# Seven half-size products in place of eight in the second mixer's output projection

## What is computed

```python
y = rms_norm(y * jax.nn.silu(z), ssm_norm_g)
mix = jnp.concatenate([y, att], axis=-1) @ w_out
x = x + g1 * mix
h = rms_norm(x, norm_ffn_g[i]) * (1 + sc2) + sh2
x = x + g2 * swiglu(h, ffn_w_gate[i], ffn_w_up[i], ffn_w_down[i])
```

## Time and profile before

| | us |
|---|---|
| runs shown, median of 3 | 1491.78 |
| lowest and highest of them | 1487.80, 1494.51 |
| profiled execution | 1488.53 |
| its span, first to last instruction | 1486.8 |
| output projection, first to last matmul (824.04 to 907.82) | 83.8 |
| mean granted clock of TensorE | 0.98 of full speed |

### The profile page before, as it was taken

The page is one execution under the profiler, slowest core; times in us unless marked ns, Lnnn a source line. Parts: engine busy times, 40 slices in busy tenths (PEclk is TensorE's granted clock), DMA queues, the critical chain, the costliest instruction groups (busy, mean ns, idle before and its releaser), DMA issues. The chain is left out here.

```text
span 1486.8 us, 18918 instructions
## 1 busy us (share of the span) xinstructions
PE 1396.1 (94%) x7609; PEld 1031.1 (69%) x7609; DVE 765.1 (51%) x1333; ACT 248.3 (17%) x530; POOL 254.1 (17%) x342
## 2 busy tenths in 40 slices
PE   5999999988677999999999999999999999999997
PEld 1877655644344888778888888777766868777774
DVE  2458775423214676844452113788763963544532
ACT  2121212000002212313343101000002022000001
POOL 5078010000002000643345104000021000000000
PEclk9999999999989999999999999999999999999999
DMA  9976788999999688847764454988843633445430
GB/s 349 314 256 236 257 339 356 378 414 418 417 417 309 226 293 289 286 123 187 172 134 136 148 162 155 330 322 334 311 170 114 203 102 114 147 165 170 155 128 28
DMA packets 176054, 355.56 MB, mean 239 GB/s; under 512 B 7289, under 2 KB 137040, under 8 KB 158560
## 3 DMA queue, kind: packets, MB, share of 16 engines
q1 hardware_dynamic: 166720, 313.64, 59.5%
q0 software_dynamic: 9248, 40.71, 9.4%
HBM read 352.58 MB, written 1.74 MB: 238 GB/s over the span
## 5 line engine op out<-in xcount | busy, mean ns | idle before, releaser
L1789 PE MATMUL PS<-HT,ring 128*128 128x256 f32 x1152 | 258.3, 382 | 0.1
L1789 PEld LDWEIGHTS PS<-HT,ring 128*128 128x128 f32 x1152 | 215.4, 190 | 36.0 <-issue 7.9
L2604 PE MATMUL PS<-ring,hid 128*128 128x512 f32 x320 | 143.5, 592 | 0.0
L2604 PEld LDWEIGHTS PS<-ring,hid 128*128 128x128 f32 x320 | 60.8, 190 | 60.3 <-issue 58.4
L2598 PE MATMUL PS<-HT,ring 128*128 128x256 f32 x464 | 101.6, 379 | 0.0
L2598 PEld LDWEIGHTS PS<-HT,ring 128*128 128x128 f32 x464 | 87.8, 190 | 11.8
L1969 PE MATMUL PS<-ring,y_T 128*128 128x256 f32 x384 | 83.3, 379 | 0.0
L1969 PEld LDWEIGHTS PS<-ring,y_T 128*128 128x128 f32 x384 | 72.9, 190 | 9.9
L1262 PE MATMUL PS<-ring_extra,slot_rows 128*32 128x256 f32 x576 | 54.2, 429 | 27.1 <-DMA ring_extra<-in_expert_w_gate 7.1
L1539 DVE TENSOR_TENSOR X<-X,PS 128x1024 f32<-128x1024 f32 x14 | 17.1, 1221 | 110.9 <-PE PS L1315 110.9
L2627 PE MATMUL PS<-ada_stage,half_sums 128*128 128x256 f32 x288 | 68.1, 379 | 0.0
(11 more groups left out here) (598 smaller groups left out, 2167.0 us busy)
## 6 DMA issues: line engine op xcount, KB each, us to landing
ring<-in_hy_w_in SPq DMA_DIRECT2D x40, 1024.0 KB, 7.6
ring_extra<-in_w_ada SPq DMA_DIRECT2D x24, 1024.0 KB, 7.9
ada_stage<-in_ada_w POOLq DMA_DIRECT2D x24, 1024.0 KB, 7.7
ring<-in_ffn_w_gate SPq DMA_DIRECT2D x22, 1024.0 KB, 5.7
ring<-in_ffn_w_up SPq DMA_DIRECT2D x22, 1024.0 KB, 5.8
ring<-in_ffn_w_down SPq DMA_DIRECT2D x22, 1024.0 KB, 5.6
ring_extra<-in_expert_w_down SPq DMA_DIRECT2D x18, 1024.0 KB, 22.9
ring_extra<-in_expert_w_up SPq DMA_DIRECT2D x18, 1024.0 KB, 20.2
```

Source lines behind the costliest of these rows:

```text
L1789: mm = pe.matmul(dst, w[:, k, half * P:(half + 1) * P], HT[:, k, :], start=(k == 0), stop=(k == KT - 1))
L2604: mm = pe.matmul(PS[:, 4 + 2 * i + h, :], hid[:, par, f, i * P:(i + 1) * P], w[:, f, h * 512:(h + 1) * 512], start=first and f == 0, stop= ...
```

## The change

The projection is done by column pieces twice as wide (`pc` = 0, 1, of 512 columns) and for each group of 1024 rows as a 2x2 block product: the rows' two token halves against the two 512-row halves, and the two 256-column halves of the weights. Seven products `P1` to `P7` of one 128x512 by 512x256 block each take the place of the eight of the plain way. What follows from that:

- DVE sums blocks of `YT` (`sum_y`, four operations of 128x512 for each group, three times) and blocks of the two weight tiles of a group (`sum_out`, four operations of 128x1024, six times; one result is written over half of a ring slot).
- PE does, for each `pc`, the attention group's products by themselves (`out_half(pc, 0)`, 28 matmuls) and those of groups 0 and 1 together, product by product (`out_half(pc, 1)`, 56 matmuls). Each product has half a PSUM bank; part 0 takes banks 2 to 5, part 1 banks 6, 7, 0 and 1.
- The four matmuls for the squares stand between the first two parts, and their result in bank 1.
- ACT copies `P1` of each part. DVE adds the products up: `combine_a` for the attention group, with gate and addition to `X`; `combine_b` for the other two, with the token's scale and the gate in one operation, in four pieces of 128x256. ACT squares `X` piece by piece.
- PE waits for the sums (`y_summed`, `out_summed`) and, before it reuses banks, for DVE to have read them (`read_a`, `read_b`). Tiles of the second column half are asked for in another order, and slots come free at other places (`used`).
- Three of `sum_y`'s and `sum_out`'s calls stand on DVE among steps 37 and 38, ahead of the multiplications of `y`; the others behind step 39.

```diff
-    segment("hy_out", [kp(hy_out[g * D:(g + 1) * D, :], c * CW) for c in range(4) for g in (2, 0, 1)])
+    OUT_GROUPS = (2, 0, 1)
+    segment("hy_out", [kp(hy_out[g * D:(g + 1) * D, :], (2 * pc + h) * CW) for pc in range(2)
+                       for g, h in ((2, 0), (2, 1), (0, 0), (1, 0), (0, 1), (1, 1))])
...
-        ta = W[:].rearrange("p a b -> p (a b)")[:, 0:2 * 512].rearrange("p (a n) -> p a n", a=2)
+        ta = W[:].rearrange("p a b -> p (a b)")[:, 0:4 * CW].rearrange("p (i n) -> p i n", i=TT)
+        partial = rx_zb[:, 0:6 * CW].rearrange("p (a n) -> p a n", a=6)
+        out_sum0 = sb(scope, "out_sums", [P, 3, 4, CW])
+        out_sum = (out_sum0[:], carve(rows_q, 0, [3, 4, CW]), carve(x_scores, 0, [3, 4, CW]))
+        y_sum = (KTT[:].rearrange("p a s -> p (a s)").rearrange("p (j k n) -> p j k n", j=4, k=4),
+                 V[:].rearrange("p i n -> p (i n)").rearrange("p (j k n) -> p j k n", j=4, k=4),
+                 carve(cum_bias, 0, [4, 4, P]))
...
+        SEVEN = ("P2", "P1", "P6", "P5", "P3", "P7", "P4")
+        OUT_ORDER = {(0, 0): SEVEN, (0, 1): ("P2", "P1", "P3", "P7", "P5", "P6", "P4"), (1, 0): SEVEN, (1, 1): SEVEN}
+        HOMES = ({"P2": (2, 0), "P1": (2, 1), "P6": (3, 0), "P5": (3, 1), "P3": (4, 0), "P7": (4, 1), "P4": (5, 0)},
+                 {"P2": (6, 0), "P1": (6, 1), "P6": (7, 0), "P5": (7, 1), "P3": (0, 0), "P7": (0, 1), "P4": (1, 0)})
+        OUT_PIECES = ((0, 0), (0, 1), (1, 1), (1, 0))
+        def out_items(n):
+            pc, gi = n // 3, n % 3
+            return tuple(OUT + 6 * pc + at for at in ((0, 1), (2, 4), (3, 5))[gi])
+
+        def y_block(g, i, h):
+            return YT[:, g * KT + 4 * h:g * KT + 4 * h + 4, i * P:(i + 1) * P]
...
-                for c in range(4):
-                    n = base + NP + 3 * c
-                    arrive(pe, n)
-                    if c == 0:
-                        pe.wait_ge(moved_att, KT)
-                        pe.wait_ge(evac, NP - 1)
-                    elif c == 1:
-                        pe.wait_ge(evac, NP)
-                    else:
-                        pe.wait_ge(part_a, c - 1)
-                    for i in range(TT):
-                        mm = out_half(n, 2, i, c % 2, True, True)
-                    mm.then_inc(used, 1)
-                    if c == 0:
-                        pe.wait_ge(copied, 2 * ATT_SLOTS)
-                    if c >= 2:
-                        pe.wait_ge(summed_out, c - 1)
-                    if c == 0:
-                        pe.wait_ge(gained, 8)
-                    for i in range(TT):
-                        for g in range(2):
-                            if i == 0:
-                                arrive(pe, n + 1 + g)
-                            mm = out_half(n + 1 + g, g, i, 6 + c % 2, g == 0, g == 1)
-                            if i == TT - 1:
+                def out_half(pc, part):
+
+                    order = OUT_ORDER[pc, part]
+                    sets = [3 * pc + gi for gi in ((0,), (1, 2))[part]]
+                    operands = {name: [] for name in order}
+                    for n in sets:
+                        g, ys, ws = OUT_GROUPS[n % 3], y_sum[n % 3], out_sum[n % 3]
+                        w0, w1 = (w_slot(item) for item in out_items(n))
+                        for name, lhs, rhs in (("P2", y_block(g, 0, 1), w0[:, 4:8, :]), ("P1", y_block(g, 0, 0), w0[:, 0:4, :]),
+                                               ("P6", ys[:, 1], ws[:, 1]), ("P5", ys[:, 0], ws[:, 0]),
+                                               ("P3", ys[:, 3], w1[:, 4:8, :]), ("P7", ys[:, 2], w1[:, 0:4, :]),
+                                               ("P4", y_block(g, 1, 1), ws[:, 2])):
+                            operands[name] += [(lhs[:, k, :], rhs[:, k, :]) for k in range(4)]
+                    summed = [name for name in order if name not in ("P2", "P1", "P3")][0]
+                    free = order[max(order.index("P3"), order.index("P7")) + 1]
+                    for n in sets:
+                        arrive(pe, out_items(n)[0])
+                    pe.wait_ge(y_summed, sets[-1] % 3 + 1)
+                    for name in order:
+                        if name == "P3":
+                            for n in sets:
+                                arrive(pe, out_items(n)[1])
+                        if name == summed:
+                            pe.wait_ge(out_summed, sets[-1] + 1)
+                        if (pc, part, name) == (0, 1, "P4"):
+                            pe.wait_ge(meaned, 1)
+                        pairs_in = operands[name]
+                        for j, (lhs, rhs) in enumerate(pairs_in):
+                            mm = pe.matmul(out_home(part, name), lhs, rhs, start=(j == 0), stop=(j == len(pairs_in) - 1))
+                            if name in (summed, free) and j < len(sets):
                                 mm.then_inc(used, 1)
-                    if c == 0:
-                        pe.wait_ge(sq_added, 8)
-                        for i in range(TT):
-                            for a in range(2):
-                                mm = pe.matmul(PS[:, 2, i:i + 1], sq_sum[:, a * S + i * P:a * S + (i + 1) * P], ones[:, 0:1],
-                                               start=(a == 0), stop=(a == 1))
-                        mm.then_inc(msum, 1)
+                        mm.then_inc(out_products, 1)
+                pe.wait_ge(moved_att, KT)
+                pe.wait_ge(copied, 2 * ATT_SLOTS)
+                out_half(0, 0)
+                pe.wait_ge(evac, NP)
+                pe.wait_ge(sq_added, 8)
+                for i in range(TT):
+                    for a in range(2):
+                        mm = pe.matmul(PS[:, 1, S + i:S + i + 1], sq_sum[:, a * S + i * P:a * S + (i + 1) * P], ones[:, 0:1],
+                                       start=(a == 0), stop=(a == 1))
+                mm.then_inc(msum, 1)
+                out_half(0, 1)
+                pe.wait_ge(read_a, 1)
+                out_half(1, 0)
+                pe.wait_ge(read_b, 1)
+                out_half(1, 1)
+                pe.wait_ge(read_a, 2)
                 keep_clock(pe, 3, 6)
...
-                                       accum_out=stat[:, 8 + 4 * i + c:9 + 4 * i + c])
-
-                for c in range(4):
-                    act.wait_ge(used, base + NP + 3 * c + 1)
-                    if c >= 2:
-                        act.wait_ge(summed_out, c - 1)
-                    act.activation(ta[:, c % 2, :], PS[:, c % 2, :], ACT.Copy).then_inc(part_a, 1)
-                    if c >= 2:
-                        square_x(c - 2)
-                square_x(2)
-                square_x(3)
+                def square_x(pc, at):
+                    i, c = OUT_PIECES[at][0], 2 * pc + OUT_PIECES[at][1]
+                    act.wait_ge(x_out, 4 * pc + at + 1)
+                    act.activation(HT[:, 2 * c + i, :], X[:, i, c * CW:(c + 1) * CW], ACT.Square,
+                                   accum_out=stat[:, 8 + 4 * i + c:9 + 4 * i + c])
+
+                for pc in range(2):
+                    for part in range(2):
+                        act.wait_ge(out_products, out_done(pc, part, "P1"))
+                        if pc:
+                            act.wait_ge((read_a, read_b)[part], pc)
+                        act.activation(partial[:, part, :], out_home(part, "P1"), ACT.Copy).then_inc(part_a, 1)
+                    for at in range(4):
+                        square_x(pc, at)
...
+                def sum_y(gi):
+                    if gi:
+                        dve.wait_ge(gained, 4 * gi)
+                    g, ys = OUT_GROUPS[gi], y_sum[gi]
+                    a11, a12, a21, a22 = (y_block(g, i, h) for i in range(TT) for h in range(2))
+                    step(dve.tensor_tensor(ys[:, 0], a21, a22, ALU.add))
+                    step(dve.tensor_tensor(ys[:, 2], a11, a21, ALU.subtract))
+                    step(dve.tensor_tensor(ys[:, 1], ys[:, 0], a11, ALU.subtract))
+                    dve.tensor_tensor(ys[:, 3], a12, ys[:, 1], ALU.subtract).then_inc(y_summed, 1)
+
+                def sum_out(n):
+                    for item in out_items(n):
+                        dve.wait_ge(landed[slots[item]], 16 * turns[item])
+                    if n >= 3:
+                        dve.wait_ge(out_products, out_done(0, min(n % 3, 1), "P4"))
+                    w0, w1 = (w_slot(item) for item in out_items(n))
+                    t1, t2, t4 = (out_sum[n % 3][:, j] for j in range(3))
+                    step(dve.tensor_tensor(t1, w1[:, 0:4, :], w0[:, 0:4, :], ALU.subtract))
+                    step(dve.tensor_tensor(t2, w1[:, 4:8, :], t1, ALU.subtract))
+                    step(dve.tensor_tensor(w1[:, 0:4, :], w1[:, 4:8, :], w1[:, 0:4, :], ALU.subtract))
+                    dve.tensor_tensor(t4, w0[:, 4:8, :], t2, ALU.subtract).then_inc(out_summed, 1)
+
+                def out_terms(pc, part):
+
+                    def product(name):
```

(83 more changed lines are left out.)

22 lines of the change are left out of this document (11 added, 11 removed).

## The result

| | before | after |
|---|---|---|
| median of the runs compared (us) | 1491.78 (1487.8 to 1494.51) | 1476.41 (1474.04 to 1480.21) |
| ratio of the times, 95% interval | | 0.9903 [0.9877, 0.993] |
| profiled execution: time, span (us) | 1488.53, 1486.8 | 1474.04, 1472.3 |
| PE busy, matmul records | 1396.1, 7609 | 1382.5, 7561 |
| DVE busy (us) | 765.1 | 811.6 |

The change makes the kernel faster by 15.4 us in the medians and by 14.5 us between the two profiled executions; the forecast was 11.1. The forecast's 11.1 us are a ratio of 0.9926, inside the first two of the three intervals and outside the third: the forecast was somewhat too small.

The account below looks back on a forecast made before the run. PE alone was taken to bound the projection (83.8 us). Fewer matmuls (10.4 us) plus a shorter tail (0.7) make 11.1 us, forecast 1480.5 us, 0.75% faster; own range 1475 to 1485, 8-in-10 range 1474.5 to 1487.5.

Parts of the forecast that it names:

- PE's work: Projection: matmuls fall from 192 to 168 at an unchanged 0.432 us each, saving 10.4 us if PE never waits.
- PE doesn't wait: Projection: every DVE sum is done before PE asks for it; smallest slack 5.0 us, in part (0,1); 6.0 in (1,1).
- POOL beside the sums: Ahead of the projection: POOL may slow beside DVE's sums, but even standing still its backlog fits; no delay taken.
- rival 1: Projection: DVE becomes the bound and PE waits for `out_summed`; gain vanishes near 1.9 times longer DVE operations; chance 0.17.
- The tail: Projection's end to the next block's first DVE instruction: 3.05 us in place of 3.76, PE's drain last; gain 0.7 us.
- The next layer costed at nothing: Behind the barrier: same code, PE's pause 0.7 us shorter, next layer's first tiles in time; counted as nothing.
- DVE's work: Step 37 to the projection's end: DVE some 65 us busier with sums, additions and gates, hidden behind PE.
- DVE as the bound: Inside the projection: longer DVE operations stall PE at 23.3 and 56.1 us, leaving no difference that shows; chance 0.17.
- The clock falls by short products: Projection: pauses between short products drop TensorE's clock; half the matmuls at the lower level give 1517 us; chance 0.05.
- The next layer gives it back: Next layer's start: held by PE's last dummy matmul or first tiles' load, time 1488 us or more; chance 0.02.

Follow-up runs that it names:

- eighth_product: Changed kernel with the four matmuls of `P4` run a second time, unread, in each of six groups (24 matmuls more): 1489.21 us, 1.0002 of the kernel before.
- sums_late_4: Changed kernel with the first weight sum of `sum_out(1)` done four times more, 5.0 us of DVE work: 1475.85 us.
- sums_late_8: Changed kernel with the first weight sum of `sum_out(1)` done eight times more, 10.0 us of DVE work: 1483.45 us, 0.9942 of the kernel before.
- no_dummies: Changed kernel without the six dummy matmuls at the end of the projection: 1481.21 us, 0.9921 of the kernel before.
- before_pool_waits: Kernel before, with POOL starting `tap_blocks` only when all of DVE's accumulations are done: 1487.43 us, 0.9981 of the kernel before.
- after_third: Changed kernel unchanged, timed again in a third comparison: 1474.78 us, 0.988 of the kernel before.
- after_again: Changed kernel unchanged, timed again: 1478.04 us, 0.9929 of the kernel before.

## Why the prediction was right, and where it was off

**PE's work: right.** 168 matmuls at 0.432 and the squares make 73.4 us, forecast 73.3, measured 73.41 or 73.42 in all seven kernels with these matmuls and no wait among them. *eighth_product* gives all of it back with the 24 matmuls alone. The pitch of the earlier trace rows was the right one to borrow, since it came from products of the same form on a busier DVE.

**PE doesn't wait: right, with the slacks.** In the trace the second weight sum of (0,1) is done 18.1 us after the start (forecast 18.3) and asked for at 23.3: slack 5.2, forecast 5.0. The one of (1,1) has 6.0, as forecast. Their last operation on DVE and the product on PE that asks for it, for (0,1) and for (1,1):

```profile
842.18 1.23 DVE L2188 TENSOR_TENSOR x_scores<-ring,x_scores 128x1024 f32<-128x1024 f32 x1
874.29 1.23 DVE L2188 TENSOR_TENSOR x_scores<-ring,x_scores 128x1024 f32<-128x1024 f32 x1
```

```profile
848.68 1.89 PE L2027 MATMUL PS<-ring,att_v 128*128 128x256 f32 x8
881.49 1.89 PE L2027 MATMUL PS<-rows_q,att_v 128*128 128x256 f32 x8
```

*sums_late_4* and *sums_late_8* bracket the first slack.

**POOL beside the sums: the bound held, the size was off.** I took no delay of the last gain, with 1.2 as the most that a row showed. In the trace both sides stretched more:

```profile
807.50 1.64 DVE L2175 TENSOR_TENSOR att_k<-att_k,y_T 128x512 f32<-128x512 f32 x1
```

```profile
808.58 3.29 POOL L2534 TENSOR_SCALAR y_T<-y_T,ssm_gain 128x256 f32<-128x256 f32 x2
...
828.85 1.82 POOL L2534 TENSOR_SCALAR y_T<-y_T,ssm_gain 128x256 f32<-128x256 f32 x2
```

A row sum took 1.64 for 0.69 and a gain pair 3.29 for 1.83. That is 2.4 and 1.8 times, so the 1.2 that I set against rival 1 was too low. It did no harm because the backlog was gone by the last round: its gain ends at 830.67, 5.33 after the projection's start, forecast 5.3, and with POOL done the sums behind it, on which the slack rests, ran at 0.69 and 1.23 as priced. What the forecast had right was to cost POOL at a standstill and find that even this fits.

**The tail: right.** 3.06, forecast 3.05, with PE's drain the last one. *no_dummies* shows the other term too: with ACT as the last one it takes 2.55, where I had worked out a gain of 1.3, that is 2.46.

**The next layer costed at nothing: this was the step that was off.** I counted nothing behind the barrier. The profiled execution gained 1.35 us there, by the clock behind the pause, 2.05 by the collision that went away, and 1.35 at the last norm; 1.30 was lost ahead of the projection. So 11.1 forecast, 11.07 measured in its two terms, and 14.5 in all. Of the rest, the 2.05 goes with the change, by way of its number of instructions: no accumulation on DVE stood in any of the five kernels with 7561 records that leave POOL's start as it is, and one stood in the kernel before both times, and *before_pool_waits* shows its worth in the time. It isn't the seven products as such that free DVE, for *no_dummies* has them and has the collision too. The two of 1.35 can't be put down to the change: the first was gone again in *after_third*; the second held in all three profiles of the changed kernel and in neither of the kernel before, but came and went in other kernels with the same pause. I had written that the pause gets 0.7 shorter and stopped there, without asking what the clock does behind it, although the trace of before had 3.10 us for these 16 transposes and 2.06 for the same ones of another norm, at 1141.66.

**DVE's work: a slip.** I expected DVE to be some 65 us busier from the first sums to the end. The same stretch, before and after:

```profile
804.10:910.50 106.40, 106.40 (x498) 93.48 (x496) 12.13 (x22) 10.59 (x27) 12.28 (x12) 1.00 0.47 150
```

```profile
805.40:900.60 95.20, 95.20 (x447) 83.91 (x446) 65.31 (x94) 10.82 (x29) 15.58 (x12) 1.00 0.52 167
```

It does 65.3 us there in all, but it is 53.2 busier: I hadn't taken off the work that the change removes. The time doesn't hang on it.

**The rivals.** *DVE as the bound* didn't happen; by *sums_late_8* it would have cost more than I priced it at, since the clock falls behind a wait. *The clock falls by short products* didn't happen either: 1.00 in all four stretches, with products of four matmuls in the parts (0,0) and (1,0), of eight in the others, and another half of a bank for each. The Trainium skill, TensorE: Matmul & The Clock Gate, section "A second HAM failure mode: psum-queue depth-cycling", tells of a clock that swung as PE idled briefly between groups of matmuls. The trace has no such pauses in this form, and a clock of 1.00, so it doesn't test what they would do. Where the clock did fall in a projection it was behind a real pause, in *sums_late_8* behind 4.69 us. *The next layer gives it back* came out with the other sign.

**What stays open.** How one packet of instructions makes the load land 3.4 us later; what beside the length makes the clock fall behind a pause of 1.9 us. The 1.30 us ahead of the projection I put down to the execution: the changed kernel's projection starts at 825.34 here, at 823.50 in *after_again* and at 826.55 in *after_third*, and over all fourteen profiles it starts anywhere from 823.19 to 829.83. The spread between the three comparisons, 0.988 to 0.9929, is not explained by these places alone.

## What to carry to other kernels

Trading an eighth of the matmuls for sums on another engine paid here by the matmuls' pitch, 24 x 0.432 us, as PE never waited. To know that ahead, lay out both engines' work from the start of the stage, find the one sum with the smallest slack, and test that one by making it late. Price a wait on PE at more than its length if the clock can fall behind it (6.65 us for a wait of 4.69 here). And a change that shifts when instructions and loads arrive moves collisions far behind it: look in the trace of before for single instructions that take several times their usual length, since these are the times that may go or come.

## What was not expected of the hardware

- A DVE accumulation with both inputs in SBUF stood still for the 7.5 us of POOL's operations (9.97 for 2.35), or POOL for DVE (9.11 for 7.54); row sums and gain pairs stretched each other from 0.69 to 1.64 and from 1.83 to 3.29.
- The landing of one 1024 KB load, 8.0 to 8.4 or 11.6 to 12.3 us, went with whether a packet of instructions (0.02 MB) came 5.1 to 5.5 us behind its issue or not; the place of that packet goes with the number of PE's instructions ahead of it, not with the time that they take.
- A pause of 1.91 to 1.95 us on PE left the clock full in some executions and not in others; one of 2.66 us or more behind this barrier never left it full, nor did the 4.69 us of *sums_late_8*.
- A matmul of one column still took 0.22 us (78.77 - 73.41 over 24), half of the 0.432 of 256 columns, as the four on the squares had it (0.81).
